# Output slots as plain fp32 pieces and norms by token half in a two-block fp32 kernel on one Trainium2 core

## The reference, cut

```python
u = rmsnorm_2(h, mix_norm_w);  p = u @ w_in
o_dn = deltanet_group(p[..., :DN_COLS], ...)   # 8 heads of 128: chunked delta rule,
                                              # o = rmsnorm_2(o, norm_w) * silu(z)
o_rw = rwkv7_group(p[..., DN_COLS:], ...)     # 16 heads of 64: wkv7 scan, then per head
                                              # (y - mean) * rsqrt(var + eps) * ln_w + ln_b
                                              # (y + bonus) * gate
h = h + concatenate([o_dn, o_rw]) @ w_out     # 2048 x 2048
h = h + memory_cross_attention(rmsnorm_2(h, xa_norm_w), rmsnorm_2(mem, mem_norm_w), wq, wk, wv, wo)
h = h + squared_relu_mlp(rmsnorm_2(h, ffn_norm_w), w1, w2)
return rmsnorm_2(h, final_norm_w)
```

## Time and profile before

| What | Value |
|---|---|
| median of three runs | 3873.78 us (3871.59 to 3874.62) |
| the profiled execution | 3873.07 us |
| its span | 3871.3 us |
| PE busy | 3602.2 us, 93% |
| DVE busy | 2361.2 us, 61% |
| ACT busy | 1507.8 us, 39% |
| POOL busy | 123.7 us, 3% |
| DMA | 650.39 MB, mean 168 GB/s |

### The profile page before, as it was taken

The page is one execution under the profiler, slowest core; times in us unless marked ns, Lnnn a source line. Parts: engine busy times, 40 slices in busy tenths (PEclk is TensorE's granted clock), DMA queues, the critical chain, the costliest instruction groups (busy, mean ns, idle before and its releaser), DMA issues.

```text
span 3871.3 us, 52424 instructions
## 1 busy us (share of the span) xinstructions
PE 3602.2 (93%) x21522; PEld 3193.3 (82%) x21522; DVE 2361.2 (61%) x2607; ACT 1507.8 (39%) x1293; POOL 123.7 (3%) x120
## 2 busy tenths in 40 slices
PE   8997799999999999999999999876868989999998
PEld 8986599999988888888888999864757878888887
DVE  3544546977767775666667663366475456666666
ACT  3333333345534333333334343334332344333333
POOL 2000000000000000000000000011111000000000
PEclk8998899999999999999999999987887999999999
DMA  4551345556676775556565454301013435555553
GB/s 177 174 195 66 120 163 172 203 187 219 224 268 234 244 248 202 200 198 205 200 204 190 153 170 168 121 1 44 24 65 114 169 120 188 191 187 192 185 193 142
DMA packets 122890, 650.39 MB, mean 168 GB/s; under 512 B 10736, under 2 KB 43888, under 8 KB 49552
## 3 DMA queue, kind: packets, MB, share of 16 engines
q1 hardware_dynamic: 116224, 620.20, 46.1%
q0 software_dynamic: 6544, 28.44, 2.0%
HBM read 620.81 MB, written 27.79 MB: 168 GB/s over the span
## 4 chain that ended last, share of the span: by engine, by line
PE 87%; DVE 9%; ACT 2%; issue 1%; DMA 0%; ACTq 0%; DVEq 0%; SPq 0%; PEldq 0%
PE pairs L2443 20%; PE pairs L2444 19%; PE pairs L2445 19%; PE quad L2488 12%; PE quad L2489 6%; DVE w_low L2188 2%; PE quad L2529 1%; PE quad L3012 1%; PE pairs L2614 1%; DVE arena L2081 1%; ACT w_high L1197 0%; PE quad L2596 0%; PE quad L2854 0%; PE quad L2901 0%; PE quad L2935 0%
## 5 line engine op out<-in xcount | busy, mean ns | idle before, releaser
L2188 DVE TENSOR_TENSOR w_low<-ring,w_high 128x2048 fp32r<-128x2048 f32 (+1 forms) x547 | 1252.6, 2291 | 931.3 <-ACT w_high L1197 930.8
L1197 ACT CAST w_high<-ring 128x2048 fp32r<-128x2048 f32 (+1 forms) x547 | 1039.7, 1901 | 1737.2 <-PE pairs L2445 1275.5
L2443 PE MATMUL pairs<-x_t,w_high 128*128 128x256 f32 x2592 | 743.9, 287 | 19.9 <-DVE w_low L2188 11.3
L2444 PE MATMUL pairs<-x_t,w_high 128*128 128x256 f32 x2592 | 737.3, 284 | 0.0
L2445 PE MATMUL pairs<-x_t,w_low 128*128 128x256 f32 x2592 | 737.2, 284 | 0.0
L2488 PE MATMUL quad<-x_t,w_high 128*128 128x512 f32 x1984 | 703.4, 399 | 9.9 <-DVE w_low L2188 9.9
L2443 PE MATMUL pairs<-w_high,act_high 128*128 128x512 f32 x1568 | 612.1, 390 | 5.4 <-ACT arena L759 3.5
L2444 PE MATMUL pairs<-w_low,act_high 128*128 128x512 f32 x1568 | 611.4, 390 | 0.0
L2445 PE MATMUL pairs<-w_high,act_low 128*128 128x512 f32 x1568 | 611.0, 390 | 0.0
L2489 PE MATMUL quad<-x_t,w_low 128*128 128x256 f32 x1984 | 557.6, 281 | 0.0
L2443 PEld LDWEIGHTS pairs<-x_t,w_high 128*128 128x128 f32 x2592 | 501.7, 194 | 22.6 <-DVE w_low L2188 11.8
(11 more groups left out here) (548 smaller groups left out, 3159.6 us busy)
## 6 DMA issues: line engine op xcount, KB each, us to landing
ring<-pu SPq DMA_DIRECT2D x128, 1024.0 KB, 4.9
ring<-pv SPq DMA_DIRECT2D x128, 1024.0 KB, 4.8
ring<-f SPq DMA_DIRECT2D x128, 1024.0 KB, 4.8
ring<-win SPq DMA_DIRECT2D x48, 1024.0 KB, 4.8
ring<-dn SPq DMA_DIRECT2D x32, 1024.0 KB, 4.8
ring<-rw SPq DMA_DIRECT2D x24, 1024.0 KB, 4.7
ring<-wout SPq DMA_DIRECT2D x16, 1024.0 KB, 4.8
ring<-wq SPq DMA_DIRECT2D x16, 1024.0 KB, 4.8
```

The costliest lines, as they stand in the source:

```text
L1197: nc.scalar.copy(WH[s % 2][:, 0:w], flat(ring[s])[:, 0:w]).then_inc(ev["split_high"], 1)
L2188: v.tensor_tensor(WL[s % 2][:, 0:w], flat(ring[s])[:, 0:w], WH[s % 2][:, 0:w].bitcast(F32), ALU.subtract).then_inc(ev["split_low"], 1)
L2443: mm(out, stat[0], mov[0], start=start, stop=False, skip_group_check=True)
L2444: mm(out, stat[0], mov[1], start=False, stop=False, skip_group_check=True)
```

## The change

It changes only the second block, from the first recurrence to the key product of the cross attention.

- **Pieces.** All 16 output slots are plain fp32 products on the loaded weights and on `YT`, unsplit. `out_pieces(q, first, n)` issues products `first` to `first + n` of the eight of slot `q` (4 row groups by 2 token tiles). `out_slot`, `out_high`, `out_low`, `OHI`, `OLO`, `YH`, `YL`, `OH1`, `OL1` and the split output slots go. Slots are ordered anew: 0 to 7 as before (`kt` 0 to 7); 8 to 11 are the four column blocks on `kt` 8 to 11, which the first half of the second recurrence gives; 12 to 15 the four on `kt` 12 to 15. Twelve slots run before the end of the last solve.
- **Places.** Half 0: slot 0 in three parts around the spread and the bonus, slot 1 before the decayed operands; 2, 3 in the substitution; slot 4 in single pieces in the waits of the solve and after the first turned tile, slot 5 around the second. Half 1: the same with 6, 7; 8, 9; 10; 11. Slots 12 to 15 after it, with the memory rows turned between them in three goes.
- **Loads.** Slots 0 to 13 alternate between ring buffers 0 and 1; 14 and 15 have two buffers in the arena. The memory rows go to ring buffers 2 and 3 (`MEMX`), loaded by SP at the start; GpSimd loads their weights early and weights them in half 0's solve, ScalarE squares them after half 0's inverse, `diagonal` stands in half 0's norm.
- **Output norm of the first recurrence by token tile:** squares, sums, root, scaling (one three-operand operation per head), turn and copy of tile 0 run while tile 1 is computed. Turned rows go straight to `YT`. The right side of tile 1 takes its factor into its operands (`DST[:, 11]`, and `VT[:, 1]` multiplied early).
- **Group norm by token tile** inside the solve, in both halves; gate, bonus, `lnw`, `lnb` are folded ahead (`BON = (BON + lnb) * GATE`, `GATE = GATE * lnw`).
- **Smaller:** `roots()` ahead of the l2 root; the key norm's root ahead of `ka_out`; a Gram pair waits for `gram_diag` where it waited for `gram_out`; additions per token tile.

The diff, cut to its core:

```diff
+        OW = ring[0:2] + [sb(f"o_late{i}", AR0 + 2048 * i, 2048)[:, :].rearrange("p (k n) -> p k n", k=4) for i in range(2)]
-        MEMX = av(16384, NT, D)
+        MEMX = sb("mem_rows", 8192, NT * D)[:, :].rearrange("p (t d) -> p t d", t=NT)
+        FINAL = (2, 3, 0, 1)
@@ stage2_loads
+            o_load(0)
+            o_load(1)
+            for t in range(NT):
+                sp.dma_start(MEMX[:, t, :], a["mem"][t * P:(t + 1) * P, :]).then_inc(ev["mem_in"], 16)
+            for q in range(2, 12):
+                sp.wait_ge(ev["o2_used"], q - 1)
+                o_load(q)
+            sp.wait_ge(ev["gram_out"], 32)
+            o_load(14)
+            sp.wait_ge(ev["inv_new"], 42)
+            o_load(15)
+            for q in (12, 13):
+                sp.wait_ge(ev["o2_used"], q - 1)
+                o_load(q)
@@ stage2_pool, in half 0 after inverse_pool
+                    pool.wait_ge(ev["mem_w_in"], 16)
+                    pool.wait_ge(ev["squared"], 2 + 8 + 16 + 2)
+                    for t in range(NT):
+                        o.tell(nc.gpsimd.tensor_tensor(MEMX[:, t, :], MEMX[:, t, :], MEMW, ALU.mult), ev["mem_weighted"])
@@ stage2_act
             act.wait_ge(*nth("dn_sq", 1))
+            roots()
             act.wait_ge(*nth("l2_mm", 1))
@@ rw_act, after inverse_act
+            if hf == 0:
+                act.wait_ge(ev["mem_in"], 32)
+                for t in range(NT):
+                    o.done(nc.scalar.activation(av(0, D), MEMX[:, t, :], ACT.Square, accum_out=SS[:, t:t + 1]), ev["squared"])
+            for t in range(NT):
+                n = 2 * hf + t + 1
+                act.wait_ge(ev["gn_mean"], n)
+                o.tell(nc.scalar.activation(RY2[:, t, :], RY[:, t, :], ACT.Square), ev["gn_sq"])
+                if t == 0:
+                    nc.scalar.activation(SM[:, 8:9], EPSC, ACT.Sqrt)
+                act.wait_ge(ev["gn_sum"], n)
+                o.tell(nc.scalar.activation(RST[:, 1, 8 * t:8 * t + 8], ...), ev["gn_root"])
@@ rw_dve, after inverse_dve
+            solved(0)
+            for j in range(J):
+                ins = v.scalar_tensor_tensor(BON[:, j, :], BON[:, j, :], col2("lnb", J * hf + j), GATE[:, j, :], ALU.add, ALU.mult)
+            o.done(ins)
+            removed(0)
+            for j in range(J):
+                ins = v.tensor_scalar(GATE[:, j, :], GATE[:, j, :], col2("lnw", J * hf + j), None, ALU.mult)
+            o.done(ins)
+            centred(0)
+            solved(1)
+            spreads(0)
+            removed(1)
+            normed(0)
+            centred(1)
+            gated(0)
+            spreads(1)
+            with_bonus(0)
+            normed(1)
+            if hf == 0:
+                diagonal()
+            gated(1)
+            with_bonus(1)
@@ stage2_pe, after both halves
+            pe.wait_ge(ev["rw_done"], 4)
+            for i in range(4):
+                if i >= 2:
+                    pe.wait_ge(ev["dve_free"], DVE0["out2"] + i - 1)
+                out_pieces(pe, mm, 12 + i, 0, 8)
...
+                if i < 3:
+                    turned_rows(4, MEMX, ((0, 1, 2), (3, 4, 5), (6, 7))[i])
@@ out_pieces
+                ins = mm(o_bank(q)[:, t], YT[:, kt0 + k, t * P:(t + 1) * P], OW[o_buffer(q)][:, k, :],
+                         start=opens and k == 0, stop=closes and k == 3, skip_group_check=True)
@@ rw_pe
+            out_pieces(pe, mm, (0, 6)[hf], 0, 2)
             pe.wait_ge(ev["lora_out"], 3 * hf + 2)
             pe.wait_ge(ev["kk_inv"], hf + 1)
...
+            out_pieces(pe, mm, (0, 6)[hf], 2, 5)
...
+            out_pieces(pe, mm, (0, 6)[hf], 7, 1)
+            out_pieces(pe, mm, (1, 7)[hf], 0, 8)
...
+                    pe.wait_ge(ev["gram_diag"], 16 * hf + m0 - 2)
...
+            for q in ((2, 3), (8, 9))[hf]:
+                out_pieces(pe, mm, q, 0, 8)
             inverse_pe(pe, mm, 1 + hf, GR[:, :, 0, :], RTI, RTT)
+            q = (4, 10)[hf]
...
+                if t == 1:
+                    out_pieces(pe, mm, q, 2, 1)
...
+                out_pieces(pe, mm, q, 3 * t, 1)
...
+                out_pieces(pe, mm, q, 3 * t + 1, 1)
...
+            turned_y(0)
+            out_pieces(pe, mm, q, 5, 3)
+            out_pieces(pe, mm, q + 1, 0, 3)
+            turned_y(1)
+            out_pieces(pe, mm, q + 1, 3, 5)
```

More of the change, by code:

```diff
@@ L1753, in inverse_dve, with stage2_dve @@
             dve.wait_ge(ev["inv_new"], 14 * (c + 1))
-        def stage2_dve(dve, o, v, half, freed, norm, turn_out_y, add_pair, low, lows):
+        def stage2_dve(dve, o, v, half, freed, norm, add_pair, low, lows):
             rows, weigh, total, diagonal = norm
@@ L1902, in stage2_dve, with head_sums, head_scales, scaled @@
             o.done(v.tensor_copy(flat(SD), PQ[:, 0:2, :].rearrange("p a b -> p (a b)")), ev["s_out"])
+            def head_sums(t):
+                dve.wait_ge(*nth(f"od_sq{t}", 1))
+                o.done(v.tensor_reduce(DST[:, 0, t, :], OSQ[t], AX.X, ALU.add), ev["od_sum"])
+            def head_scales(t):
+                dve.wait_ge(*nth(f"od_root{t}", 1))
+                o.done(v.reciprocal(DST[:, 0, t, :], DST[:, 1, t, :]))
+            def scaled(t):
+                if t == 0:
+                    dve.wait_ge(*nth("z_silu", 1))
+                for h in range(DH):
+                    c = slice(h * P, (h + 1) * P)
+                    ins = v.scalar_tensor_tensor(OD[:, t, c], OD[:, t, c], DST[:, 0, t, h:h + 1], ZT[:, t, c], ALU.mult, ALU.mult)
+                o.tell(ins, ev["tp_scaled"])
@@ new lines, in stage2_dve, with final_add @@
+            y_second(0)
+            head_sums(1)
+            head_scales(1)
+            dve.wait_ge(ev["od_ready"], 1)
+            scaled(1)
+            y_second(1)
+            for hf in range(2):
+                rw_dve(dve, o, v, hf, diagonal)
+            def final_add(i):
+                dve.wait_ge(ev["o2_used"], 13 + i)
+                cols = slice(BLK * FINAL[i], BLK * (FINAL[i] + 1))
+                for t in range(NT):
+                    ins = v.tensor_tensor(X[:, t, cols], X[:, t, cols], o_bank(12 + i)[:, t], ALU.add)
+                freed(ins)
@@ new lines, in normed, with tile, gated @@
+            def normed(t):
+                dve.wait_ge(ev["gn_root"], n + t + 1)
+                o.done(v.reciprocal(stat(2, t), stat(1, t)))
+                o.done(v.tensor_tensor(heads(RY, t), heads(RY, t), bc(stat(2, t), 64), ALU.mult), ev["gn_out"])
+            def tile(x, t):
+                return x[:, :, t * P:(t + 1) * P]
+            def gated(t):
+                dve.wait_ge(ev["ry_turned"], n + t + 1)
+                o.done(v.tensor_tensor(tile(YT[:, y0:y0 + J, :], t), PQ[:, t, :].rearrange("p (j s) -> p j s", j=J), tile(GATE, t),
+                                       ALU.mult))
@@ L2241, in _ @@
             norm = (rows, weigh, total, diagonal)
-            def turn_out_y(low, high, weight):
-                low, high = (x[:, :].rearrange("p (k t) -> p k t", k=8) for x in (low, high))
-                for t in range(NT):
-                    for g in range(2):
-                        dve.wait_ge(ev["y_high"], 2 * t + g + 1)
-                        tile = (slice(None), slice(4 * g, 4 * g + 4), slice(t * P, (t + 1) * P))
-                        o.tell(v.scalar_tensor_tensor(low[tile], PQ[:, g, :].rearrange("p (n t) -> p n t", n=4), weight,
-                                                      high[tile].bitcast(F32), ALU.mult, ALU.subtract), ev["y_out"])
             def add_pair(name, j, slots=4):
@@ L2398, in _ @@
             peer_dve(dve, o, v, low)
-            stage2_dve(dve, o, v, half, freed, norm, turn_out_y, add_pair, low, lows)
+            stage2_dve(dve, o, v, half, freed, norm, add_pair, low, lows)
         def mlstm_pe(pe, mm):
@@ L2944, in rw_pe, with turned_y @@
                     pe.wait_ge(ev["ry_out"], n)
[L2945 to L2948 removed]
+            def turned_y(t):
+                pe.wait_ge(ev["gn_out"], 2 * hf + t + 1)
                 for j in range(J):
```

359 lines of the change are left out of this document (136 added, 223 removed), and 1 row of the table STEPS.

## The result

The changed kernel takes 3809.4 us (median of four runs, 3804.36 to 3810.16), the kernel before 3874.2 beside it: ratio 0.9831, 95% interval 0.9814 to 0.9848. The profiled execution took 3810.16 us, with a span of 3808.3.

The account below looks back on a forecast made before the run. The prediction saw no steady bound in this stretch, only a chain of short steps between engines with TensorE idle 103 of 411 us. Its terms summed to −54.7 us, from 3873.8 to 3819 us, range 3800 to 3840.

Parts of the forecast that it names:

- rival (e): Whole change slower: plain products become the bound, 20 us more TensorE work; 3898 us, chance 0.03.
- Items 1 to 3: Before the lora products: early root table −1.3, second token half's factor applied earlier −1.2, output norm by half −7.3 us.
- Items 4 and 5: Lora products to key norm's spread, −3.7 and −6.2 us by half; Gram products waiting only for the mask, −1.2 each half.
- Item 6: Slots 2, 3, 8, 9 in the substitution: hidden in the first half, +0.7 us in the second.
- Item 7: Pieces in both solves' waits: first +4.3 to −9.9, second +3.4 to −15.2 us; middles −2.8 and −5.9 taken.
- Items 7 and 8: First solve: pieces in its waits −2.8 us, GpSimd's weighting of the memory rows moved there +1.0 us.
- Rival (c): First solve: GpSimd holds VectorE's bonus operations twice, +5.8 us instead of +1.0; 3824 us, chance 0.07.
- Item 9: End of the first solve to the second half's lora products: turned rows and eleven pieces, −0.6 us.
- Item 10: After the second solve to the last output product: 73 us becomes 48.1, −25 us; −26.8 at full clock.
- rival (d): After the second solve: output slots 12 and 13 wait some 3 and 4 us for loads; 3826 us, chance 0.05.
- Rival (a): Both solves stay at low clock: total gain −36.7 us, 3837 us, chance 0.27.
- rival (b): Full clock throughout, −9.9 and −15.2 us in the solves: total gain −74.7 us, 3799 us, chance 0.14.

Follow-up runs that it names:

- experiment 5: On the changed kernel, 22 of the 32 pieces of slots 0, 1, 6 and 7 beside the decay stage left out: 3809.0 us.
- experiment 6: On the kernel of experiment 1, the middle four pieces of each of slots 2, 3, 8 and 9 beside the substitution left out: 3795.2 us.
- experiment 7: On the changed kernel, the early load of the square root table ahead of the l2 sums undone: 3811.5 us.
- experiment 1: On the changed kernel, GpSimd's weighting moved from the first solve to behind the decayed operands, ScalarE's squares ahead of the output norm: 3796.8 us, again 3794.5.
- experiment 4: On the kernel of experiment 1, two pieces of slot 3 and three of slot 9 moved behind the inverse's first two groups: 3794.6 us.
- experiment 3: On the kernel of experiment 1, only the first piece of each solve taken out, the others moved up one place: 3801.5 us.
- experiment 2: On the changed kernel, the five pieces of slots 4 and 10 taken out of the solves and issued behind the first turned rows: 3832.9 us.
- experiment 8: On the kernel of experiment 1, slot 8 moved ahead of the second half's decayed operands, slots 10 and 11 moved up: 3788.2 us.

## Why the prediction was right, and where its sizes were off

**The bound.** Idle gaps in a chain, not TensorE's work, set the stretch: 18.8 and 13.7 us of plain products fewer gained nothing (experiments 5 and 6), and rival (e) is ruled out.

**Items 1 to 3.** Item 1 is worth 3.0 us and not 1.3, but the changed kernel's profiled execution has none of it (experiment 7). From the inverse's product L2662 to the lora products the kernel before takes 60.5 us, experiments 1, 5 and 7 take 51.7 and the changed kernel 52.7; so items 2 and 3 are −8.8 us where −8.5 stood, less 1.0 for the clock in that execution.

**Items 4 and 5.** The key norm's two terms are within 0.2 us. The Gram item brought 1.5 of its 2.4 us. The row it was taken from has 1.6 us in all; the 0.8 on top, for latency, did not come.

**Item 6** gave −1.9 and +2.0 where 0 and +0.7 stood. Nearly all of both is the clock behind the first wait of the inverse, which the item left out; a dip there costs 1.6 us (experiment 4). The kernel before dipped in the first half and not in the second, the changed kernel the other way round. At equal clock the traces give −0.3 (45.3 instead of 45.6) and +0.4 (44.4 instead of 44.0), so the item's terms were about right, and that the two dips cancel in the sum is chance.

**Item 7, second solve,** is the largest miss: −15.9 where −5.9 was taken. Both bounds were worked out rightly, 24.3 us at full clock against 23.6 measured. The wrong step was to take the middle of two levels for a solve whose waits are all filled: it ran at full clock for all 24 us in every trace. Times between the bounds do occur, but with a wait open (26.3 us at 0.87 in experiment 3) or after an early fall (28.1 us at 0.82 in experiment 4). Of the rows that I weighed, 4.20 busy of 6.00 us at full clock pointed to the high end and the 50 us at 0.50 to the low one; neither had a 512 column piece in it.

**Items 7 and 8, first solve,** gave +1.6 where −1.8 stood. Rival (c), held at 0.07, happened. Its mechanism was named rightly, its price was not: I counted +5.8 for two holds, the bonus operation became 8.5 us longer, and the clock lost behind the stall added 4. Without GpSimd the solve is 23.6 us, so the hold and the low clock behind it took back 12.2 us. The row of 5.79 us was one hold; two GpSimd operations back to back hold for 9.36 us, and nothing spoke for VectorE slipping out between. The value of 1.0 rested on an order of 0.2 us. All four traces with the weighting in this place (the changed kernel and experiments 2, 5 and 7) show 10.16 or 10.17 us, so this was no accident of one execution, and 0.07 was too low.

**Item 9** was −3.5 for −0.6: four transposes take 0.5 us at full clock, not 1.1, and since the first tile's norm lay in the solve, TensorE ran from the last solve product through eleven pieces without a wait.

**Item 10** was −26.5 for −25, near its full-clock value of −26.8. The loads never showed as a wait, so rival (d) did not occur. Rival (a) is ruled out by the second solve, rival (b) was right for that solve and wrong for the first.

So the mechanism was right, and that the total came within 10 us was partly luck. The second solve gained 10.0 us more than forecast and the first 3.4 less, because of the stall. Without the stall the same change takes 3796.8 and 3794.5 us (experiment 1), below the stated range of 3800 to 3840: the unexpected cost of GpSimd is what kept the number inside it.

## What to carry to other kernels

Look for the waits of a chain and put wide, independent matmuls into them even if they cost more TensorE time: they hide, and they keep the clock for the narrow products behind, which is worth more than the hiding. Where a clock has two levels, forecast each level as a case, with the condition that decides it, and don't take the middle. Read the same group of instructions in several traces before a difference of 1 to 5 us is given to an edit. Before a GpSimd operation is moved, list VectorE's operations with two SBUF inputs in the new place; beside operations with one of their two operands in PSUM it was free.

## What the runs showed of the hardware

- Sixteen products of 64 columns take 2.00 us or 3.68 us. A single open wait of 0.86 us ahead of them made the difference in both solves of experiment 3 (3.67 and 3.68). With a 512 column piece in that wait they took 2.00 us in 14 solves of 16.
- Two GpSimd operations over 128x2048 (9.36 us) held a VectorE operation with two SBUF inputs throughout: 10.17 us instead of 1.67. Beside VectorE's masks from PSUM the same two took 9.00 us, and the masks 0.71 each, as ever.
- An open wait in the inverse does not always cost the clock, and a filled one in the solve does not always keep it. In the first half the changed kernel and experiment 4 had no dip in the inverse and a fall at the start of the solve; the other traces with pieces in the waits had it the other way round (in experiment 6 the dip came ahead of the inverse's wait). In the second half 2.7 us of open wait cost the clock in some traces and not in experiments 3 and 8. What decides it stays open.
